# An S5 recurrence cut into chunks of four tokens, with powers of the transition in its matrices

## The chip, the cores and the metric

The kernel runs on one core of a Trainium2 chip. The metric is the device time of one execution in microseconds (us); the median of three runs of the kernel before is 2751.92 us (2749.49 to 2754.79).

## The reference

Two blocks of two layers each run over 256 tokens of width 1024. The first block has gated feed-forwards, an attention with an LRU, and a short-convolution mixer. The second block has, in each layer, a mixer of two groups (S5 and gated linear attention, GLA) and then a feed-forward (a dense one in its first layer, 8 experts with 2 chosen per token in its second). All weights are float32. The change touches the S5 group alone:

```python
# u: 256 tokens x 512 channels = 32 groups of 16 channels; 64 complex states per group
lam_bar = exp(lam * dt)                           # one complex factor per state
b_bar = ((lam_bar - 1) / lam)[..., None] * b_mat  # 64 x 16 per group
bu = einsum('gph,blgh->blgp', b_bar, u)
h[l] = lam_bar * h[l-1] + bu[l]                   # over all 256 tokens
y = einsum('ghp,blgp->blgh', c_mat, h).real + d_skip * u
y = gelu(y); y_s5 = y * sigmoid(y @ w_glu + b_glu)
```

A mixer is followed by a projection of both groups, a residual sum and a layer norm.

## The kernel before

The program is written out engine by engine with semaphores; nothing but the code's own order sets the order of the work. `SUBS` names ten stages: stages 6 and 8 (`mix2`) are the two S5 and GLA mixers, stages 5 and 7 are the feed-forwards ahead of them. Weights arrive by SP's queue in units (1 MB and 0.5 MB). ScalarE makes a rounded copy of each (`hi`, lines 395 and 402) and VectorE the rest of it (`lo_gu`, `lo_d`, lines 857 and 862), and TensorE does three products for one (`mm3`, lines 1721 to 1723). A feed-forward is a loop over such units.

A mixer goes so on TensorE (`mix2`, line 2009). First come the projections (`stream`, six units), with the eight levels of the GLA scores between them (`level`, line 2047, matrices of 64 rows that use one half of the array each, in turns). VectorE prepares each level (`differences`, `decayed`, lines 1242 to 1250) and takes it up (`masked`, lines 1258 to 1268), and does `lo` of the next units between. Then comes the recurrence, in eight rounds `r`, each of two state tiles (a tile is 128 states, that is two groups). `bu(r)` (line 2130) makes the input of the states, complex and 256 tokens long. VectorE turns it by a table `E` of powers of the transition's phase (`turn_in`, lines 1319 to 1322), joins the products (1339, 1340), scans four rows of 256 (1344) with the factor's size alone as decay, and turns back: two products on VectorE (`turn_back`, 1329 and 1330), two on GpSimd (1705, 1706). TensorE multiplies the four products with the C matrices (`CS`, line 2154, outputs of 32 rows). `skip` (1287) adds `d_skip * u`. In rounds 0 and 1 VectorE also does the GLA heads' norm (`gated_heads`, 1298; `mixed_heads`, through line 1091). TensorE puts the first row block of the projection (`r_[0]`) ahead of the last round.

GpSimd builds the tables `E` (16384 numbers a partition for 16 tiles, real and imaginary, `table`, lines 1617 to 1629) during stages 5 and 7, after the last `modulation` sums. In a mixer it fetches `s5_c`, waits for the GLA gate and multiplies it (1688), fetches the B matrices of each round (1691, 1696), and does its two products a round. `CS` is made by VectorE at the start of a mixer (1208 to 1214, seven instructions).

Of the kernel before, what the change touches and what calls it, by code (L numbers as in the profile page):

```python
# [22 lines left out]
F32 = mybir.dt.float32  # L23
# [22 lines left out]
LEVELS = (64, 32, 16, 8, 4, 2, 1)  # L46

# [52 lines left out]
def program(nc, A, out):  # L100
    with ExitStack() as ctx:
# [14 lines left out]
        XH, XL = sb("xT_hi", [P, KD, S], F32R), sb("xT_lo", [P, KD, S], F32R)  # L116
        MH, ML = sb("mixT_hi", [P, KD, S], F32R), sb("mixT_lo", [P, KD, S], F32R)
# [32 lines left out]
        def view(at, n):  # L150
# [12 lines left out]
        E = view(8192, 8192).rearrange("p (c t s) -> p c t s", c=2, t=16)  # L163
# [32 lines left out]
        SBM = [view(1024 + 512 * i, 512).rearrange("p (c t m) -> p c t m", c=2, t=2) for i in range(2)]  # L196
        CS = view(2048, 1536).rearrange("p (c t h) -> p c t h", c=3, t=16)
        CRAW = view(3584, 1024).rearrange("p (c t h) -> p c t h", c=2, t=16)
        CT = [view(4608 + 512 * i, 512).rearrange("p (t h) -> p t h", h=32) for i in range(2)]
        W = view(3584, 1024).rearrange("p (c t s) -> p c t s", c=2, t=2)  # L200
        PP = [view(4608 + 512 * i, 512) for i in range(4)]
        TURNED = [[ROW[:, 512 * i:512 * i + 512] for i in range(4)],
                  [ROW[:, 2048:2560], HG, first_net[:, 0:512], first_net[:, 512:1024]]]
# [25 lines left out]
        s5b_in, s5c_in = [sem(f"s5b_in{i}") for i in range(2)], sem("s5c_in")  # L229
# [26 lines left out]
            "table", "bu", "bu_used", "states", "prod", "prod2", "y", "ysum", "gelu", "yh", "yl", "sig", "gated")}  # L256
# [25 lines left out]
        def s5_input(r, c):  # L282

            return PA[:, 2 * ((r + 1) % 2) + c, :]
# [5 lines left out]
        def tile2(x):  # L290

            return x.rearrange("p a b -> p (a b)")

# [95 lines left out]
        def _(act):  # L389
# [127 lines left out]
            def ffn(n0, dyn, nf):  # L517
# [7 lines left out]

                if n0 == 0:
                    steps(0)
                with act.Fori(1 if n0 == 0 else 0, nf // 2) as j:
                    steps(dyn + j * 2)
# [114 lines left out]
            def mix2(b):  # L644
# [7 lines left out]
                def keep_u(t, used, count):  # L652
                    act.wait_ge(used, count)
                    act.activation(UT[:, t, :], PA[:, t % 2, 0:S], ACT.Copy).then_inc(g["u_sb"], 1)
# [20 lines left out]
                decay(1)  # L675
                act.wait_ge(d_used, U + 3)
# [7 lines left out]
                decay(6)  # L684
                keep_u(0, gu_used, U + 5)
# [15 lines left out]
                act.activation(grs, gss, ACT.Sqrt, bias=eps_rms, scale=1.0 / P).then_inc(g["root"], 1)  # L701
# [1823 lines left out]
```

## Time and profile before

| | us |
|---|---|
| median of three runs | 2751.92 |
| span of the profiled execution | 2747.2 |
| TensorE busy in it | 2600.3 (95%) |
| VectorE busy | 2165.5 (79%) |
| ScalarE busy | 1483.6 (54%) |
| GpSimd busy | 947.8 (34%) |

The span runs from the first to the last instruction of the profiled execution; the page gives no other time of that execution, and the runs' median is 4.7 us above it. The chain that ended last is to 38% of the span TensorE's; the rest of it lies on no other engine for more than 1%. The two recurrences lie at 1136 to 1208 us and at 1566 to 1638 us. In them TensorE is busy for 51.4 of 72 us and VectorE for 70.4.

### The profile page before, as it was taken

To read this page: it belongs to the slowest core of one execution; us is meant where nothing else is said; L and a number is where in the kernel's file an instruction comes from. 1 tells how busy PE (TensorE), PEld (TensorE's weight loads), DVE (VectorE), ACT (ScalarE), POOL (GpSimd) and SP (SyncE) were. 2 spreads that over 40 slices of the span, in tenths; PEclk is the share of its full clock that TensorE was granted. 3 is DMA by queue.
4 is the path that set the end of the run, shared out by engine and by line. 5 is a ranking of instruction groups with operands and counts; after the bars stand their busy time and mean duration, and the time that the engine had idled before them with its cause. 6 is when DMAs were issued, how large, how long until landed. Compare 5 with 4: busy or idle time off the path is not lost. (4 is left out here: it accounts for less than half of the span.)

```text
span 2747.2 us, 47482 instructions
## 1 busy us (share of the span) xinstructions
PE 2600.3 (95%) x17802; PEld 2379.0 (87%) x17802; DVE 2165.5 (79%) x2488; ACT 1483.6 (54%) x1930; POOL 947.8 (34%) x586
## 2 busy tenths in 40 slices
PE   8999899999998998888998978999999999999997
PEld 7999699999897998658998747999999999999986
DVE  5667666766787676987855997898989898989888
ACT  4337543443434334424334515777777777777765
POOL 6990089688789992126900130000000000000000
PEclk9999999999999998999999988999999999999999
DMA  8664267566566653324553415999999999999985
GB/s 309 252 237 148 103 241 256 202 250 254 191 241 229 220 183 134 115 105 164 183 184 138 164 63 192 343 350 333 352 335 349 338 347 343 347 345 346 340 320 216
DMA packets 129209, 670.58 MB, mean 244 GB/s; under 512 B 14672, under 2 KB 14992, under 8 KB 80064
## 3 DMA queue, kind: packets, MB, share of 16 engines
q1 hardware_dynamic: 111024, 604.72, 59.9%
q0 software_dynamic: 18064, 64.21, 6.9%
q8 instruction: 81, 1.33, 0.2%
q14 instruction: 40, 0.33, 0.0%
HBM read 667.82 MB, written 1.05 MB: 243 GB/s over the span
## 5 line engine op out<-in xcount | busy, mean ns | idle before, releaser
L1721 PE MATMUL work<-xT_hi,wh_gu 128*128 128x256 f32 x2088 | 593.9, 284 | 21.6 <-DVE xT_lo L985 12.0
L1722 PE MATMUL work<-xT_lo,wh_gu 128*128 128x256 f32 x2088 | 592.3, 284 | 0.0
L1723 PE MATMUL work<-xT_hi,wl_gu 128*128 128x256 f32 x2088 | 591.7, 283 | 0.0
L1721 PE MATMUL work<-wh_gu,mixT_hi 128*128 128x256 f32 x1792 | 507.5, 283 | 2.8 <-DVE wl_gu L1439 1.5
L1722 PE MATMUL work<-wl_gu,mixT_hi 128*128 128x256 f32 x1792 | 505.8, 282 | 0.0
L1723 PE MATMUL work<-wh_gu,mixT_lo 128*128 128x256 f32 x1792 | 505.5, 282 | 0.0
L857 DVE TENSOR_TENSOR wl_gu<-raw_gu,wh_gu 128x2048 fp32r<-128x2048 f32 x158 | 392.3, 2483 | 72.0 <-ACT wh_gu L395 71.5
L1721 PEld LDWEIGHTS work<-xT_hi,wh_gu 128*128 128x128 f32 x2088 | 401.3, 192 | 30.1 <-issue 21.3
L1722 PEld LDWEIGHTS work<-xT_lo,wh_gu 128*128 128x128 f32 x2088 | 401.7, 192 | 4.8
L1723 PEld LDWEIGHTS work<-xT_hi,wl_gu 128*128 128x128 f32 x2088 | 401.5, 192 | 0.0
L862 DVE TENSOR_TENSOR wl_d<-raw_d,wh_d 128x1024 fp32r<-128x1024 f32 x157 | 250.2, 1594 | 189.6 <-ACT wh_d L402 189.5
L1721 PE MATMUL acc<-wh_d,h_hi 128*128 128x512 f32 x912 | 380.4, 417 | 2.8 <-DVE wl_d L1444 2.7
L1723 PE MATMUL acc<-wh_d,h_lo 128*128 128x512 f32 x912 | 361.2, 396 | 0.0
L1722 PE MATMUL acc<-wl_d,h_hi 128*128 128x512 f32 x912 | 361.1, 396 | 0.0
L1721 PEld LDWEIGHTS work<-wh_gu,mixT_hi 128*128 128x128 f32 x1792 | 340.9, 190 | 12.5 <-DVE wl_gu L1439 1.7
L1722 PEld LDWEIGHTS work<-wl_gu,mixT_hi 128*128 128x128 f32 x1792 | 341.6, 191 | 8.8
L1723 PEld LDWEIGHTS work<-wh_gu,mixT_lo 128*128 128x128 f32 x1792 | 341.5, 191 | 0.0
L402 ACT ACTIVATE wh_d<-raw_d 128x1024 fp32r<-128x1024 f32 x157 | 166.2, 1059 | 276.1 <-PE acc L1723 276.1
L395 ACT ACTIVATE wh_gu<-raw_gu 128x2048 fp32r<-128x2048 f32 x158 | 300.7, 1903 | 25.4 <-PE acc L1723 25.0
L1652 POOL TENSOR_SCALAR scratch<-scratch,small 128x1024 f32<-128x1024 f32 x84 | 312.9, 3724 | 4.2
L1439 DVE TENSOR_TENSOR wl_gu<-raw_gu,wh_gu 128x2048 fp32r<-128x2048 f32 x113 | 259.1, 2293 | 38.0 <-ACT wh_gu L726 37.9
L1439 DVE TENSOR_TENSOR wl_gu<-scratch,wh_gu 128x2048 fp32r<-128x2048 f32 x112 | 256.6, 2291 | 25.5 <-ACT wh_gu L726 25.0
(436 smaller groups left out, 4785.6 us busy)
## 6 DMA issues: line engine op xcount, KB each, us to landing
raw_gu<-in_w_gu SPq DMA_DIRECT2D x271, 1024.0 KB, 5.2
raw_d<-in_w_d SPq DMA_DIRECT2D x269, 512.0 KB, 5.4
scratch<-in_w_gu SPq DMA_DIRECT2D x112, 1024.0 KB, 7.2
scratch<-in_w_d SPq DMA_DIRECT2D x112, 512.0 KB, 7.8
scratch<-in_w_mod POOLq DMA_DIRECT2D x96, 512.0 KB, 3.7
scratch<-in_s_b POOLq DMA_DIRECT2D x16, 256.0 KB, 2.9
rows<-in_norm_post POOLq DMA_DIRECT2D x6, 512.0 KB, 4.4
rows<-in_ln_g POOLq DMA_DIRECT2D x4, 512.0 KB, 5.5
```

The costliest lines, as they stand in the source:

```text
L395: act.activation(wh_gu[k][:, :, :, :].rearrange("p a k n -> p (a k n)"), raw_gu[k][:, :], ACT.Copy).then_inc(gu_hi, 1)
L402: act.activation(wh_d[k][:, :], raw_d[k][:, :], ACT.Copy).then_inc(d_hi, 1)
L857: TT(wl, raw_gu[k][:, :], wh.bitcast(F32), ALU.subtract).then_inc(gu_lo, 1)
L862: TT(wl_d[k][:, :], raw_d[k][:, :], wh_d[k][:, :].bitcast(F32), ALU.subtract).then_inc(d_lo, 1)
L1439: TT(wl, RAW_GU[k] if k > 1 else RAW_GU[k][:, :], wh.bitcast(F32), ALU.subtract).then_inc(gu_lo, 1)
L1652: link(pool.tensor_scalar(MW[n % 3], MW[n % 3], c, None, ALU.mult))
L1721: pe.matmul(out_, w[0], m[0], start=start, stop=False)
L1722: pe.matmul(out_, w[0], m[1], start=False, stop=False)
L1723: return pe.matmul(out_, w[1], m[0], start=False, stop=stop)
```

## The change

`PH` = 4 tokens form a chunk, so there are `NC` = 64 chunks. The 256 tokens are kept by phase: ScalarE writes `u` as 4 blocks (phase) of 64 (chunk) (`keep_u`), and the output is put back in order when the mixer's result is written.

- The input of a chunk's state is the sum over its four tokens of (power of the transition) times B times u. GpSimd makes the powers of B in the feed-forward ahead (`input_powers`, 18 operations of 128 x 512), from rows that TensorE has spread out there (`transition_rows`, 32 products) and ScalarE has copied. TensorE's `inputs(half)` has 64 products of 32 rows into 128, 64 columns each; the four state tiles of a set use the array's four row blocks. All of it is two halves, not eight rounds.
- The scans run over chunks with the decay's fourth power. VectorE has `states(half)` and `turn_back(half)`, operations of 1024 or 512 a partition, and one scan of 1024 (16 rows of 64, each begun afresh by a zero in the decay). ScalarE fills the decays (`decays`, 8 small operations a half).
- The output of a token is C times (power) times the state of the chunk before (`outputs(t)`, 32 products of 32 x 64 for each `t`) and a short convolution inside the chunk (`nearby(t)`, four products). Its kernel is TensorE's `kernels()` (128 products of 32 x 32), copied by ScalarE into a block form that GpSimd has zeroed (`kernel_blocks`).
- The C matrices' powers are made by GpSimd at the start of each mixer (`output_powers`, 30 operations of 128 x 512), in place of VectorE's seven, and ahead of the gate's product. GpSimd's two products a round and the B fetches in the mixer are gone; the B matrices are fetched whole, by eight DMAs, before. The table has 64 places in place of 256.

```diff
+PH = 4
+NC = S // PH
...
+                if n0 in (START[5], START[7]):
+                    ahead, l = 2, 1 + (n0 == START[7])
+                    steps(0)
+                    act.wait_ge(s["bt_ps"], l)
+                    act.activation(BST.rearrange("p c t h -> p (c t h)"), tile2(PB[:, 2:4, :]), ACT.Copy).then_inc(s["bt_sb"], 1)
+                    steps(2)
+                    act.wait_ge(s["lam_ps"], l)
+                    act.activation(LAM.rearrange("p c x -> p (c x)"), tile2(PB[:, 2:4, :]), ACT.Copy).then_inc(s["lam_sb"], 1)
...
+                    act.activation(UT[:, t, :].rearrange("p (f c) -> p f c", f=PH),
+                                   PA[:, t % 2, 0:S].rearrange("p (c f) -> p f c", f=PH),
+                                   ACT.Copy).then_inc(g["u_sb"], 1)
...
+                def decays(half):
+
+                    act.wait_ge(s["bpow"], n + 1)
+                    act.wait_ge(s["fresh"], n + 1)
+                    per = DEC[:, half].rearrange("p (j c t x) -> p j c t x", j=4, c=2, t=2)
+                    for j in range(4):
+                        for t in range(2):
+                            at = 16 * n + 8 * half + 4 * t + j
+                            last = act.activation(per[:, j, :, t, :], fresh_start.unsqueeze(1).broadcast_to([P, 2, NC]),
+                                                  ACT.Copy, scale=s5p[:, 1, at:at + 1])
+                    last.then_inc(s["dec"], 1)
...
+                def kernel_blocks():
+
+                    act.wait_ge(s["kern"], n + 1)
+                    act.wait_ge(s["kzero"], n + 1)
+                    for j in range(4):
+                        r = slice(32 * j, 32 * j + 32)
+                        act.activation(NEARBY[r, :, :, r], PB[r, 3, :].rearrange("p (t d h) -> p t d h", t=4, d=PH),
+                                       ACT.Copy).then_inc(s["kd"], 1)
...
-                TT(CT[0], CRAW[:, 0], cr, ALU.mult)
-                link(TT(CT[1], CRAW[:, 1], ci, ALU.mult))
-                TT(CS[:, 0], CT[0], CT[1], ALU.subtract)
-                link(TT(CS[:, 1], CT[1], CT[0], ALU.subtract))
-                TT(CT[0], CRAW[:, 0], ci, ALU.mult)
-                link(TT(CT[1], CRAW[:, 1], cr, ALU.mult))
-                link(STT(CS[:, 2], CT[0], -1.0, CT[1], ALU.mult, ALU.subtract))
...
+                def states(half):
+
+                    er, ei = turn(half)
+                    v, w, wa, wb = s5_input(half), pairs(W), pairs(WA), pairs(WB)
+                    dve.wait_ge(s["bu"], 2 * n + half + 1)
+                    if half == 0:
+                        dve.wait_ge(s["table"], n + 1)
+                    TT(wa, v, er, ALU.mult)
+                    link(TT(wb, v, ei, ALU.mult))
+                    TT(w[:, :, 0], wa[:, :, 0], wb[:, :, 1], ALU.add).then_inc(s["bu_used"], 1)
+                    link(TT(w[:, :, 1], wa[:, :, 1], wb[:, :, 0], ALU.subtract))
+                    dve.wait_ge(s["dec"], 2 * n + half + 1)
+                    dve.tensor_tensor_scan(W, DEC[:, half], W, 0.0, ALU.mult, ALU.add).then_inc(s["states"], 1)
...
+                def turn_back(half):
+
+                    er, ei = turn(half)
+                    w, wa, wb = pairs(W), pairs(WA), pairs(WB)
+                    dve.wait_ge(s["states"], 2 * n + half + 1)
+                    TT(wa, w, er, ALU.mult)
+                    link(TT(wb, w, ei, ALU.mult))
...
+                    TT(h[:, 0, :, :, 1:NC], cut[0][:, :, 0], cut[1][:, :, 1], ALU.subtract)
+                    link(TT(h[:, 1, :, :, 1:NC], cut[0][:, :, 1], cut[1][:, :, 0], ALU.add))
+                    dve.memset(small[:, 4:5], 0.0).then_inc(s["prod"], 1)
+
+                states(0)
+                gated_heads()
+                turn_back(0)
+                states(1)
+                mixed_heads()
+                turn_back(1)
+                skip(0)
+                skip(1)
                 lo_gu(U + 7)
+                skip(2)
                 skip(3)
                 lo_d(U + 7)
...
+            def input_powers(n):
+
+                pool.wait_ge(s["lam_sb"], n + 1)
+                pool.wait_ge(s5b_in, 128 * (n + 1))
+                lr, li = LAM[:, 0], LAM[:, 1]
+                t = ET[:, 0:512]
+                for k in range(1, PH):
+                    (r0, i0), (r1, i1) = ((BP[:, x, 0], BP[:, x, 1]) for x in (k - 1, k))
+                    TT(r1, r0, lr, ALU.mult)
+                    link(TT(t, i0, li, ALU.mult))
+                    link(TT(r1, r1, t, ALU.subtract))
+                    TT(i1, r0, li, ALU.mult)
+                    link(TT(t, i0, lr, ALU.mult))
+                    link(TT(i1, i1, t, ALU.add))
...
+            def output_powers(n):
+
+                def of(i):
+                    return s5p[:, i, 16 * n:16 * n + 16].unsqueeze(2).broadcast_to([P, 16, 32])
+                cr, ci, t = CRAW[:, 0], CRAW[:, 1], CTMP
+                pool.wait_ge(s5c_in, 16 * (n + 1))
+                for d in range(PH + 1):
...
+                    b0, b1 = CP[d - 1][:, 0], CP[d - 1][:, 1]
+                    TT(c0, b0, of(0), ALU.mult)
+                    link(TT(t, b1, of(18), ALU.mult))
+                    link(TT(c0, c0, t, ALU.add))
+                    TT(c1, b1, of(0), ALU.mult)
+                    link(TT(t, b0, of(18), ALU.mult))
+                    link(TT(c1, c1, t, ALU.subtract))
+                    if d >= PH - 1:
+                        pool.memset(small[:, 6:7], 0.0).then_inc(s["cpow"], 1)
...
+                    output_powers(n)
...
+            def input_columns(n):
+
+                pe.wait_ge(s5b_in, 128 * (n + 1))
+                for c in range(2):
+                    for t in range(4):
+                        last = pe.transpose(PB[:, 2 + c, t * P:(t + 1) * P], BP[:, 0, c, t * P:(t + 1) * P], ident)
+                last.then_inc(s["bt_ps"], 1)
+
+            def transition_rows(n):
+
+                pe.wait_ge(par_ready, 1)
+                for c, i in enumerate((0, 18)):
+                    for t in range(4):
+                        for j in range(4):
+                            at = 16 * n + 4 * t + j
+                            last = pe.matmul(PB[32 * j:32 * j + 32, 2 + c, t * P:(t + 1) * P],
+                                             s5p[:, i, at:at + 1].broadcast_to([P, 32]), ident, start=True, stop=True)
...
+                ahead = 0
+                if n0 in (START[5], START[7]):
+                    ahead, l = 1, int(n0 == START[7])
+                    input_columns(l)
+                    for r in (2, 3):
+                        gate_up(n0 + r)
+                        down(n0 + r - 1, 0, f0 + r - 1, 0, False, False)
+                    pe.wait_ge(s["bt_sb"], l + 1)
+                    transition_rows(l)
...
+                def inputs(half):
+
+                    if half == 0:
+                        pe.wait_ge(s["bpow"], n + 1)
...
+                    for t in (2 * half, 2 * half + 1):
+                        for c in range(2):
+                            for f in range(PH):
+                                for j in range(4):
+                                    r, at = slice(32 * j, 32 * j + 32), (4 * c + t) * NC
+                                    last = pe.matmul(PA[:, j, at:at + NC], BP[r, PH - 1 - f, c, t * P:(t + 1) * P],
+                                                     UT[r, t, f * NC:(f + 1) * NC], start=f == 0, stop=f == PH - 1)
                     last.then_inc(s["bu"], 1)
 
-                bu(0)
+                def kernels():
+
+                    pe.wait_ge(s["bt_sb"], n + 1)
+                    pe.wait_ge(s["cpow"], 2 * n + 1)
+                    for t in range(4):
+                        for d in range(PH):
+                            for c in range(2):
+                                for j in range(4):
+                                    at = (PH * t + d) * 32
+                                    last = pe.matmul(PB[32 * j:32 * j + 32, 3, at:at + 32], BST[:, c, 4 * t + j, :],
+                                                     CP[d][:, c, 4 * t + j, :], start=c == 0, stop=c == 1)
+                    last.then_inc(s["kern"], 1)
+
+                def nearby(t):
+
+                    for d in range(PH):
+                        pe.matmul(s5_output(t)[:, d * NC:S], NEARBY[:, t, d, :], UT[:, t, 0:S - d * NC], start=d == 0, stop=False)
+
+                def outputs(t):
+
+                    half = t // 2
+                    pe.wait_ge(s["prod"], 2 * n + half + 1)
+                    for f in range(PH):
+                        for c in range(2):
+                            for j in range(4):
+                                last = pe.matmul(s5_output(t)[32 * j:32 * j + 32, f * NC:(f + 1) * NC],
+                                                 CP[f + 1][:, c, 4 * t + j, :], HS[half][:, c, 2 * j + t % 2, :],
+                                                 start=False, stop=(f, c) == (PH - 1, 1))
+                    last.then_inc(s["y"], 1)
+
+                r_ = [row_of(k) for k in (6, 7, 4, 5, 3, 0, 1, 2)]
+                inputs(0)
                 heads()
-                bu(1)
+                kernels()
+                inputs(1)
...
+                nearby(0)
+                nearby(1)
+                outputs(0)
+                outputs(1)
+                pe.wait_ge(mix_l, MSTART[b] + 2)
+                nearby(2)
+                nearby(3)
+                pe.wait_ge(gu_lo, U + 7)
+                pe.wait_ge(s["bu_used"], 2 * (n + 1))
+                r_[0](U + 6, 0).then_inc(gu_used, 1)
+                outputs(2)
+                outputs(3)
```

TensorE in the first mixer, from the last GLA level (line 2047) on; before, word for word (`rows` are the scores or the turned products, `acc` and `work` the two halves of PSUM):

```order
L2047 MATMUL work<-scratch 128x128 x8
L2130 MATMUL acc<-scratch 128x256 x4
L2105 MATMUL work<-rows 128x128
L2106 MATMUL work<-rows 128x128
L2107 MATMUL work<-rows 128x128
...
L2130 MATMUL acc<-scratch 128x256 x4
L2114 MATMUL work<-const,scratch 128x128 x8
L2130 MATMUL acc<-scratch 128x256 x4
L2154 MATMUL work<-rows,scratch 32x256 x8
L2130 MATMUL acc<-scratch 128x256 x4
L2154 MATMUL work<-rows,scratch 32x256 x2
L2154 MATMUL work<-const,scratch 32x256 x2
```

Three rounds' inputs went ahead of the first outputs. Now, at the same place (line 2179 is the last GLA level, 2262 `inputs`, 2237 to 2239 the heads, 2275 `kernels`, 2246 the heads' transposes, 2282 `nearby`, 2291 `outputs`):

```order
L2179 MATMUL work<-scratch 128x128 x8
L2262 MATMUL acc<-scratch 128x64 x64
L2237 MATMUL work<-rows 128x128
...
L2275 MATMUL work<-scratch,mixT_hi_plain 32x32 x24
L2275 MATMUL work<-mixT_lo_plain,mixT_hi_plain 32x32 x8
...
L2262 MATMUL acc<-scratch 128x64 x64
L2246 MATMUL work<-const,scratch 128x128 x8
L2282 MATMUL work<-scratch 128x256
L2282 MATMUL work<-scratch 128x192
...
L2291 MATMUL work<-rows,scratch 32x64 x16
L2291 MATMUL work<-rows,mixT_lo_plain 32x64 x8
L2291 MATMUL work<-rows,mixT_hi_plain 32x64 x8
```

What were 4 products of 256 columns a round are now 64 of 64 columns a half, and the 128 small products of the kernels stand between the two halves' inputs.

GpSimd at the start of the first mixer, before:

```order
L1630 MEMSET small 128x1
L1682 DMA rows<-in_head_gain 128x512
L1683 DMA w_alpha<-in_w_alpha 16x256
L1685 DMA scratch<-in_s_c 128x1024
L1688 TENSOR_TENSOR const<-const,rows 128x1024
L1691 DMA scratch<-in_s_b 128x512 x2
L1696 DMA scratch<-in_s_b 128x512
```

And now (1795 to 1798 are the same three fetches; 1724 to 1737 are `output_powers`, of which the first seven operations stand here):

```order
L1795 DMA rows<-in_head_gain 128x512
L1796 DMA w_alpha<-in_w_alpha 16x256
L1798 DMA scratch<-in_s_c 128x1024
L1799 MEMSET scratch 128x64
L1800 MEMSET scratch 128x1
L1724 TENSOR_TENSOR scratch<-scratch,s5p 128x512
L1725 TENSOR_TENSOR mixT_lo_plain<-scratch,s5p 128x512
L1726 TENSOR_TENSOR scratch<-scratch,mixT_lo_plain 128x512
L1727 TENSOR_TENSOR scratch<-scratch,s5p 128x512
L1728 TENSOR_TENSOR mixT_lo_plain<-scratch,s5p 128x512
L1729 TENSOR_TENSOR scratch<-scratch,mixT_lo_plain 128x512
L1732 TENSOR_TENSOR scratch<-scratch,s5p 128x512
```

Nothing stood between the fetch of C and the gate's product (line 1688 before); now 30 operations of 128 x 512 do.

## Rows read from the trace of the kernel before

**Rows 1.** Stretches: length, busy us (count) of PE, PEld, DVE, ACT, POOL; clock, DMA:

```profile
937.00:1048.00 111.00, 111.00 (x783) 104.01 (x783) 83.55 (x67) 42.26 (x39) 105.38 (x114) 1.00 0.54 189
1074.00:1136.00 62.00, 61.78 (x452) 54.33 (x452) 49.59 (x78) 34.47 (x42) 4.01 (x4) 0.97 0.39 145
1136.00:1208.00 72.00, 51.41 (x241) 30.90 (x238) 70.38 (x114) 9.26 (x23) 24.09 (x22) 0.88 0.13 45
1504.00:1566.00 62.00, 61.63 (x450) 54.20 (x452) 54.17 (x82) 34.26 (x42) 5.10 (x6) 0.97 0.41 149
1566.00:1638.00 72.00, 51.37 (x242) 30.87 (x238) 70.51 (x114) 9.39 (x23) 24.07 (x22) 0.88 0.14 45
```

**Rows 2.** Waits, 1136 to 1208 us: who waited for whom, us, times, longest:

```profile
PE work L2154 <- DVE rows L1330: 13.9, 5, 3.4
```

**Rows 3.** Timeline of TensorE: start, us, operation [idle before]:

```profile
1135.02 1.16 PE L2047 MATMUL work<-scratch 64*128 64x128 f32 x16
1136.11 1.99 PE L2130 MATMUL acc<-scratch 128*128 128x256 f32 x8
1138.07 0.49 PE L2105 MATMUL work<-rows 128*128 128x128 f32 x2
...
1140.85 1.89 PE L2130 MATMUL acc<-scratch 128*128 128x256 f32 x8
1149.15 1.97 PE L2114 MATMUL work<-const,scratch 128*128 128x128 f32 x8 [6.41 <-DVE scratch L1298]
...
1201.84 0.50 PE L1721 MATMUL acc<-wh_gu,mixT_hi 128*128 128x512 f32 x1
...
1205.18 1.02 PE L2154 MATMUL work<-rows,scratch 128*32 128x256 f32 x4 [0.31 <-POOL const L1706]
```

**Rows 4.** Line 2047 alone: durations in ns, min/median/max, first and last start:

```profile
L2047 PE MATMUL work<-scratch x256: 272/272/373, 1097.2 to 1566.0; 64*128 64x128 f32 x128
```

**Rows 5.** Timeline of VectorE in the recurrence and behind it:

```profile
1140.66 0.69 DVE L1339 TENSOR_TENSOR scratch<-scratch 128x512 f32<-128x512 f32 x1
...
1141.98 2.44 DVE L1344 TENSOR_TENSOR_SCAN scratch<-s5p,scratch 128x256 f32<-128x256 f32 x4
...
1146.94 2.16 DVE L1298 SCALAR_TENSOR_TENSOR scratch<-work,small,const 128x128 f32<-128x128 f32 x8
...
1157.95 1.28 DVE L1091 TENSOR_TENSOR mixT_lo<-work,mixT_hi 128x512 fp32r<-128x512 f32 x2
...
1208.00 0.48 DVE L1287 SCALAR_TENSOR_TENSOR scratch<-scratch,cols,work 128x256 f32<-128x256 f32 x1 [0.81 <-PE work L2154]
...
1210.70 1.23 DVE L1361 TENSOR_TENSOR xT_lo<-scratch,xT_hi 128x1024 fp32r<-128x1024 f32 x1 [1.09 <-ACT xT_hi L710]
```

**Rows 6.** Timeline of GpSimd while the table is built:

```profile
984.46 1.04 POOL L1618 TENSOR_TENSOR scratch<-scratch,s5p 128x512 f32<-128x512 f32 x1
...
988.82 3.09 POOL L1621 TENSOR_TENSOR scratch<-scratch,s5p 128x512 f32<-128x512 f32 x1
991.99 1.29 POOL L1622 TENSOR_TENSOR scratch<-scratch 128x512 f32<-128x512 f32 x1
```

**Rows 7.** Timeline of VectorE in the same stretch:

```profile
987.88 3.13 DVE L857 TENSOR_TENSOR wl_gu<-raw_gu,wh_gu 128x2048 fp32r<-128x2048 f32 x1
...
992.10 1.47 DVE L1072 TENSOR_TENSOR h_lo<-scratch,h_hi 128x256 fp32r<-128x256 f32 x1
```

**Rows 8.** Timeline of VectorE in the projections of the stage:

```profile
1087.05 2.29 DVE L857 TENSOR_TENSOR wl_gu<-raw_gu,wh_gu 128x2048 fp32r<-128x2048 f32 x1 [6.63 <-ACT wh_gu L395]
...
1090.39 0.69 DVE L1208 TENSOR_TENSOR scratch<-scratch,s5p 128x512 f32<-128x512 f32 x1
...
1104.54 0.42 DVE L1249 TENSOR_TENSOR scratch<-scratch 128x256 f32<-128x256 f32 x1
```

**Rows 9.** Timeline of GpSimd, the DMA of the C matrices:

```profile
1076.01 0.55 POOL L1685 DMA_DIRECT2D scratch<-in_s_c  x1 [6.35 <-DVE xT_lo L985]
```

**Rows 10.** DMA issues: KB each, median us to landing:

```profile
scratch<-in_s_c POOLq DMA_DIRECT2D x2, 512.0 KB, 3.9
```

More of the change, by code:

```diff
@@ L684, in mix2 @@
                 decay(6)
+                decays(1)
                 keep_u(0, gu_used, U + 5)
@@ new lines, in pairs, with turn @@
+                def pairs(x):
+                    return x.rearrange("p (j c y) -> p j c y", j=4, c=2)
+                def turn(half):
+                    return (E[:, c, half].rearrange("p (j y) -> p j y", j=4).unsqueeze(2).broadcast_to([P, 4, 2, 2 * NC])
+                            for c in range(2))
+                def states(half):
[10 more added lines that the diff above has]
+                    dve.tensor_tensor_scan(W, DEC[:, half], W, 0.0, ALU.mult, ALU.add).then_inc(s["states"], 1)
@@ L1630, in table @@
-                pool.memset(small[:, 6:7], 0.0).then_inc(s["table"], 1)
+                turns = E.rearrange("p c h (o x) -> p c (h o) x", o=8)
+                pool.memset(turns[:, 0, :, 0:1], 1.0)
+                pool.memset(turns[:, 1, :, 0:1], 0.0)
+                for c, i in enumerate((11, 10)):
+                    last = pool.tensor_copy(pw[:, c].rearrange("p (h j t) -> p h j t", h=2, j=4),
+                                            s5p[:, i, 16 * n:16 * n + 16].rearrange("p (h t j) -> p h j t", h=2, t=2))
@@ new lines, in table, with squared @@
+                link(last)
+                def squared():
+                    TT(t0, pw[:, 0], pw[:, 0], ALU.mult)
+                    link(TT(t1, pw[:, 1], pw[:, 1], ALU.mult))
+                    link(TT(pw[:, 1], pw[:, 0], pw[:, 1], ALU.mult))
+                    TT(pw[:, 0], t0, t1, ALU.subtract)
+                    link(TT(pw[:, 1], pw[:, 1], pw[:, 1], ALU.add))
+                squared()
+                squared()
+                w = 1
+                while w < NC:
+                    pr, pi = (pw[:, c].unsqueeze(2).broadcast_to([P, 16, w]) for c in range(2))
+                    et = ET[:, 0:16 * w].rearrange("p (t s) -> p t s", t=16)
+                    re0, im0 = turns[:, 0, :, 0:w], turns[:, 1, :, 0:w]
+                    re1, im1 = turns[:, 0, :, w:2 * w], turns[:, 1, :, w:2 * w]
+                    TT(re1, re0, pr, ALU.mult)
+                    link(TT(et, im0, pi, ALU.mult))
+                    link(TT(re1, re1, et, ALU.subtract))
+                    TT(im1, re0, pi, ALU.mult)
+                    link(TT(et, im0, pr, ALU.mult))
+                    link(TT(im1, im1, et, ALU.add))
+                    w *= 2
+                    if w < NC:
+                        squared()
```

221 lines of the change are left out of this document (82 added, 139 removed).

## The prediction

> **What bounds the kernel now.** I read the busy time by stretch first. In the feed-forward ahead of the first mixer TensorE is busy for 111.0 of 111 us, in the projections of both mixers for 61.8 and 61.6 of 62, in the two recurrences for 51.4 of 72 only; there VectorE is busy for 70.4 and 70.5 of 72 [rows 1]. So outside the recurrences a microsecond more on TensorE is a microsecond of the kernel, and in them VectorE sets the pace. The waits say the same: in the first recurrence TensorE waits 13.9 us for VectorE's second turned product [rows 2] and 6.4 us for its gated heads [rows 3]. A recurrence lasts from 1136.11 us, the first `bu`, to 1208.48, the end of the last `skip` [rows 3, 5]: 72.4 us, and what stands behind it waits for it.
>
> **The recurrence, new: TensorE.** Let p be the time between two matmul records when small products follow each other in different parts of the array. A float32 product is two records (8 products are x16 [rows 3]). A recurrence then has 2 x 128 records of `inputs`, 256 of `kernels` and 4 x 64 of `outputs`: 768p. Beside them stand the heads, 1138.07 to 1140.85, 2.8 us; their transposes, 2.0; four `nearby`, each 640 columns, where 1024 columns took 1136.11 to 1138.07, so 1.2 each and 4.9 together; one row block, 1201.84 to 1204.87, 3.0; one `skip` at the end, 0.5 [rows 3, 5]. Sum 13.2 + 768p, against 72.4: a recurrence gets shorter by 59.2 - 768p, if TensorE is then its bound.
>
> Is it? VectorE: an operation of 512 is 0.69 us, one of 1024 is 1.23, a scan of 1024 as four of 256, 2.44 [rows 5]. `states` is 2 x 1.23 + 2 x 0.69 + 2.44 = 6.3, `turn_back` 2 x 1.23 + 2 x 0.69 and small memsets, 3.9. Behind the second `inputs` it owes 6.3 + 1.3 (`mixed_heads`) + 3.9 = 11.5 us until `outputs(2)`; TensorE has 2.0 + 4.9 + 3.0 + 128p = 9.9 + 128p to do in that time, more than 11.5 from p = 0.013 on. So VectorE falls from bound to second. ScalarE's kernel blocks and GpSimd's memset lie beside `inputs(1)`; `decays` on ScalarE, 16 small operations, lie in the projections, where it is busy for 34.5 of 62 us [rows 1]. I cost these at nothing; without that cover a few us each.
>
> What is p? No row shows four parts in turns with so few columns. The nearest is line 2047: two halves of the array in turns, 16 records from 1135.02 to 1136.11, 0.068 each with the change-over, (1.16 - 0.27) / 15 = 0.059 without [rows 3, 4]. The heads, in one part, take 2.78 / 24 = 0.116 a record. So two parts run side by side at 0.116 / 2. If four do too, p = 0.029; if the sequence of instructions is what limits, p stays at 0.059, and with change-overs 0.068. Fewer columns (32 or 64, not 128) argue for the lower end, four times as many instructions in a row as any row has for the upper. I take the middle of 0.029 and 0.059, p = 0.044: 33.8 + 13.2 = 47.0 us, so 25.4 us less for each recurrence; the ends give 36.9, 13.9 and 7.0 (at 0.068) less.
>
> A rule of the Trainium skill speaks to this. "TensorE: Matmul & The Clock Gate", section "Wait — 56ns, not 53.3ns?", has two floors for small matmuls: about 25 ns between starts, and about 62 ns for each where the engine's sequencer decodes in its software. The rows' 0.059 is between them and decides neither. By the first the sum below would come to about -43 us, by the second to +19.
>
> **New on TensorE in the feed-forwards.** Eight transposes (as the heads', 2.0 us [rows 3]) and 32 products, 64p = 2.8: 4.8 us a layer. TensorE has no idle time there [rows 1], so they count in full. Bounds 3.9 and 6.4.
>
> **New on GpSimd, and what it does to VectorE.** In the feed-forwards it loses the table's long steps and gets 18 operations; VectorE has pauses there (83.6 of 111 us busy with GpSimd busy for 105.4) and TensorE does not wait for it [rows 1]: nothing. In the mixers it is another matter. `output_powers` starts when C has landed, 1076.0 + 3.9 = 1080 [rows 9, 10], and is 20 products of 1.04 us and 10 sums of 1.29 [rows 6], 34 us if nothing is in the way. These lie on the projections, where GpSimd now works for 4 us [rows 1] and VectorE has a chain that TensorE follows closely. While the table was built the two engines held each other up: a product of GpSimd took 3.09 us in place of 1.04, while VectorE's `wl_gu` ran, itself 3.13 in place of 2.29; `h_lo`, of 256 places, took 1.47, where such an operation takes 0.42 [rows 6 to 8]. So an operation of VectorE that reads two tiles of SBUF and meets one of GpSimd waits for about 0.84 to 1.05 us. In the projections nearly all of them read two. 30 meetings of 1.0 are 30 us a layer. Against that stands VectorE's slack: 62 - 49.6 = 12.4 in the first mixer, 62 - 54.2 = 7.8 in the second, and the seven operations for `CS` that go, 7 x 0.69 = 4.8 [rows 1, 8]. Late by 30 - 17.2 = 12.8 and 30 - 12.6 = 17.4, together 30 us, and late here is late for TensorE: each level waits for `decayed`, and behind the level in its queue stand the next unit's products. Bounds: 0 if GpSimd always yields; 39 if every meeting costs the whole operation (68 - 29.8, rounded up). I take 30.
>
> **The sum**, on the profiled execution's 2747.2 us: 2 x (13.2 + 768p - 72.4) + 2 x (2.0 + 64p) + 30 = 1664p - 84.4. At p = 0.044 that is -11. The median of the runs is 4.7 us over the span; I leave that as it is: 2752 - 11 = 2741. It is nothing at p = 0.051.
>
> **Rivals.**
> - *The sequence of small instructions is the bound* (p 0.059 to 0.068, from 0.051 it decides). Place: `inputs`, `kernels` and `outputs`, 1536 records in both layers. For it: nothing in the trace goes faster for long than 0.059; against it: there two parts reach exactly twice one part's pace, so the array, not the sequence, seems to limit. The sum: +14 to +29, 2766 to 2781.
> - *Four parts run side by side* (p = 0.029): -36, 2716. For it the same exact halving.
> - *GpSimd yields* and costs VectorE some 8 us and not 30, at p = 0.044: -33, 2719. Against it 3.13 and 1.47 in the rows.
> - *The change moves the bound and gains nothing*: TensorE is by then in the recurrence for what VectorE was, within 5.5 us in all, p near 0.051.
> - TensorE's clock is granted at 0.88 in the recurrence [rows 1], so some of it at 1.2 and not 2.4 GHz. If the thin products get it for all of it, the 13.2 us of wide work in each grow by up to 13.2, less what they have now; I keep that for the upper end.
>
> **How the numbers follow.** Forecast, some -25 to -6 us: 0.34. Four parts side by side or a yielding GpSimd: 0.22. No change: 0.08. Slow sequence, with or without a slow clock: 0.36. What a measurement of this kernel tells from no change is 0.2%, 5.5 us. So faster 0.56, same 0.08, slower 0.36. The range for 8 in 10 takes in p = 0.029 with half the loss on GpSimd (-51) and p = 0.059 to 0.068 (+14 to +29): 2702 to 2778. The likeliest case has 2727 to 2747 for itself.
>
> **What would show it.** In the profile after: records of `inputs`, `kernels` and `outputs` 0.03 to 0.06 us apart; the recurrence 40 to 55 us long with TensorE nearly always at work; VectorE's short operations in the projections at 1.2 to 1.5 us, and 10 us and more of TensorE's idle time before the levels, more in the second mixer; 4 to 6 us more in each feed-forward. I am wrong if the records stand 0.06 or more apart, if VectorE's 0.42 us stay 0.42 beside GpSimd, or if VectorE's halves, not TensorE, end the recurrence.

## The result, and the profile after

The kernel before takes 2752.4 us (median of 4 runs), the changed one 2726.3 (4 runs, 2723.6 to 2730.9): a ratio of 0.9898, 95% interval 0.9883 to 0.9913, 26 us less. The forecast was 11 less. The profiled executions are 2747.2 and 2728.8 us long, 18.4 apart; these two stand at the fast end of one group of runs and at the slow end of the other.

I cut both traces at the same events: `xT_lo` of a mixer (VectorE), its first `inputs` or `bu` (TensorE), and the `xT_lo` behind its last `skip`. Lengths in us:

| stretch | before | after | difference | forecast |
|---|---|---|---|---|
| start to first mixer's `xT_lo` | 1071.81 | 1077.64 | +5.8 | +4.8 |
| projections 1 | 64.30 | 79.44 | +15.1 | +12.8 |
| recurrence 1 | 74.60 | 38.02 | -36.6 | -25.4 |
| rest of mixer 1, norm | 36.01 | 36.02 | 0.0 | 0 |
| feed-forward between | 255.24 | 267.06 | +11.8 | +4.8 |
| projections 2 | 64.28 | 83.21 | +18.9 | +17.4 |
| recurrence 2 | 74.60 | 37.86 | -36.7 | -25.4 |
| rest | 1106.41 | 1109.57 | +3.2 | 0 |

How far one profile may be trusted: until the first cut the changed kernel and six of the kernels below run the same instructions, and that stretch was 1071.3 to 1078.6 us long in their seven profiles. A few microseconds there or in the rest are no finding, the +5.8 of the first row included. Where the code is the same, the projections repeat within about 2 us, the first recurrence within 1 (37.0 to 38.0) and the second within 3 (35.1 to 37.9). The busy times by stretch, of the changed kernel (columns as in [rows 1]):

```profile
1077.64:1157.08 79.44, 65.34 (x452) 56.72 (x452) 64.93 (x75) 41.18 (x63) 48.58 (x36) 0.91 0.30 106
1157.08:1195.10 38.02, 33.97 (x858) 31.21 (x856) 29.75 (x42) 13.66 (x30) 2.92 (x3) 0.82 0.19 67
1498.17:1581.38 83.21, 67.78 (x453) 58.90 (x453) 72.57 (x79) 41.19 (x63) 47.46 (x38) 0.86 0.29 105
1581.38:1619.24 37.86, 31.22 (x858) 28.49 (x856) 29.65 (x42) 13.54 (x30) 2.92 (x3) 0.91 0.23 82
```

and the same two stretches of projections of the kernel before:

```profile
1071.81:1136.11 64.30, 61.89 (x453) 54.34 (x453) 51.89 (x82) 36.74 (x47) 4.01 (x4) 0.95 0.38 140
1501.95:1566.23 64.28, 61.87 (x452) 54.31 (x452) 56.45 (x86) 36.51 (x47) 5.10 (x6) 0.95 0.39 144
```

VectorE (third busy time) works 13 and 16 us longer in the projections, with seven operations fewer. TensorE's waits, in the projections of the first and of the second mixer (who waited for whom, us, times, longest):

```profile
PE work L2198 <- DVE scratch L1306: 7.4, 1, 7.4
PE work L2179 <- DVE scratch L1306: 3.8, 1, 3.8
...
PE work L2198 <- DVE scratch L1306: 7.2, 1, 7.2
PE work L2179 <- DVE scratch L1306: 4.7, 1, 4.7
```

Line 1306 is `decayed`, lines 2179 and 2198 the levels that follow it: 11 to 12 us of waiting a layer, none before. On VectorE a `decayed` beside a power on GpSimd, and a `differences` of the same shape after the last power (what was 0.42 us in [rows 8] is 0.42 only where GpSimd rests); then one of GpSimd's operations beside `wl_gu` (1.04 us alone, [rows 6]):

```profile
1118.34 1.26 DVE L1306 TENSOR_TENSOR scratch<-scratch 128x256 f32<-128x256 f32 x1
...
1144.62 0.42 DVE L1298 TENSOR_TENSOR scratch<-scratch 128x256 f32<-128x256 f32 x1
```

```profile
1093.14 2.98 POOL L1732 TENSOR_TENSOR scratch<-scratch,s5p 128x512 f32<-128x512 f32 x1
```

TensorE in the first recurrence (start, length, records; in brackets the idle time ahead, where "issue" means that nothing in the profile released it). This is the stretch that answers to [rows 3]:

```profile
1157.08 3.80 PE L2262 MATMUL acc<-scratch 32*128 32x64 f32 x128
...
1163.69 0.60 PE L2275 MATMUL work<-scratch,mixT_hi_plain 128*32 128x32 f32 x46
...
1167.04 0.53 PE L2275 MATMUL work<-scratch,mixT_hi_plain 128*32 128x32 f32 x38 [1.99 <-issue]
...
1170.77 6.67 PE L2262 MATMUL acc<-scratch 32*128 32x64 f32 x120 [2.06 <-issue]
1177.38 1.97 PE L2246 MATMUL work<-const,scratch 128*128 128x128 f32 x8
1179.14 3.97 PE L2282 MATMUL work<-scratch 128*128 128x256 f32 x16
1183.04 0.65 PE L2291 MATMUL work<-rows,scratch 128*32 128x64 f32 x32
```

The distance between two records is here 0.028 us in `inputs(0)` ((3.80 - 0.27) / 127, the length of the last taken off), (0.60 - 0.20) / 45 = 0.009 in `kernels`, (0.65 - 0.22) / 31 = 0.014 in `outputs`. Twice TensorE stands still for 2 us with nothing to wait for. From 1168.5 us, shortly after the first gap, to 1182.1 the granted clock is 0.50, its lower level (1.2 GHz), and behind the second gap 120 records of `inputs(1)` take 6.67 us, where at the full clock it would be 3.6:

```profile
1170.00:1177.00 7.00, 6.23 (x116) 6.23 (x120) 4.69 (x10) 2.35 (x4) 0.14 (x1) 0.50 0.02 5
```

VectorE in the same stretch ([rows 5] before):

```profile
1160.95 1.23 DVE L1378 TENSOR_TENSOR xT_hi_plain<-acc,scratch 128x1024 f32<-128x1024 f32 x1 [1.92 <-PE acc L2262]
...
1168.61 0.20 DVE L1349 RECIPROCAL small<-small 128x8 f32<-128x8 f32 x1 [1.65 <-ACT small L762]
...
1177.51 1.22 DVE L1378 TENSOR_TENSOR xT_hi_plain<-acc,scratch 128x1024 f32<-128x1024 f32 x1 [2.67 <-PE acc L2262]
...
1192.40 0.48 DVE L1343 SCALAR_TENSOR_TENSOR scratch<-scratch,cols,work 128x256 f32<-128x256 f32 x1 [0.41 <-PE work L2291]
```

From 1160.95 to the second half's turn-back at 1188.4 it has two short pauses: `inputs(1)` came 2.67 us late because of TensorE's gaps and its clock, ScalarE's root for the heads 1.65 late. TensorE waits for no other engine in this recurrence; its busy 33.97 us and the two gaps (1.99 and 2.06) are the whole 38.02. In the second recurrence it is otherwise. There TensorE has one gap, `inputs(1)` goes at the full clock in 3.87 us, and TensorE then waits for VectorE's `mixed_heads`:

```profile
1606.30 4.96 PE L2282 MATMUL work<-scratch 128*128 128x256 f32 x16 [4.63 <-DVE mixT_lo L1158]
```

So the first is as long as TensorE alone makes it, and in the second the chain goes through VectorE, at almost the same 38 us. In the feed-forward between the mixers TensorE waits for the DMAs of the second layer's B, which are issued only at 1244.68, behind `x_done` and the norm's rows:

```profile
1255.94 1.97 PE L1918 MATMUL work<-const,scratch 128*128 128x128 f32 x8 [6.46 <-DMA scratch<-in_s_b]
```

### The profile page after: what moved, and what is told of

It is laid out like the page before. It is cut to its first block, busy times and chain, and to the rows that moved or that the text cites. A ratio compares the mean times of both kernels' runs of the same rounds, so it can differ in the third digit from the quotient of the medians.

```text
span 2728.8 us, 50009 instructions
## 1 busy us (share of the span) xinstructions
PE 2581.1 (95%) x19162; PEld 2392.5 (88%) x19162; DVE 2100.9 (77%) x2330; ACT 1502.7 (55%) x1974; POOL 937.1 (34%) x590
## 4 chain that ended last, share of the span: by engine, by line
PE 77%; DVE 10%; POOL 6%; ACT 3%; issue 2%; DMA 1%; DVEq 0%; POOLq 0%; ACTq 0%
PE work L1823 15%; PE work L1824 15%; PE work L1825 15%; PE acc L1823 8%; PE acc L1825 8%; PE acc L1824 8%; POOL scratch L1761 3%; POOL scratch L1762 2%; DVE wl_gu L919 1%; PE work L2368 1%; DVE wl_d L924 1%; PE acc L2428 1%; PE work L1881 1%; DVE mixT_lo L1158 1%; PE work L1910 1%
## 5 line engine op out<-in xcount | busy, mean ns | idle before, releaser
L1823 PE MATMUL work<-xT_hi,wh_gu 128*128 128x256 f32 x2088 | 596.0, 285 | 22.5 <-DVE xT_lo L1052 12.1
L1823 PEld LDWEIGHTS work<-wh_gu,mixT_hi 128*128 128x128 f32 x1792 | 341.2, 190 | 12.8 <-DVE wl_gu L1492 1.7
L1492 DVE TENSOR_TENSOR wl_gu<-raw_gu,wh_gu 128x2048 fp32r<-128x2048 f32 x113 | 259.1, 2293 | 37.9 <-ACT wh_gu L788 37.8
```

What stands on the lines that cost most here:

```text
L1492: TT(wl, RAW_GU[k] if k > 1 else RAW_GU[k][:, :], wh.bitcast(F32), ALU.subtract).then_inc(gu_lo, 1)
L1823: pe.matmul(out_, w[0], m[0], start=start, stop=False)
```

## The experiments

**Parts in a row.** Do the parts of the array really work side by side? The same products, one part after the other:

```diff
-                            for f in range(PH):
-                                for j in range(4):
+                            for j in range(4):
+                                for f in range(PH):
```

and likewise in `kernels` and `outputs`.

> The changed kernel with the loops of inputs, kernels and outputs turned so that all products of one part of the array come one after the other, then those of the next part; the same products in the same number. Theory: the short records (0.030 us in inputs, 0.009 in kernels, 0.014 in outputs) come from four parts working side by side. In a row they are then 0.12, 0.036 and 0.056 apart; inputs(0), 3.7 us from first to last record, takes 15; the recurrence, 38 us, takes 60 to 75; the kernel about 45 to 75 us more, some 2775 to 2800. Rival: the records are short because the products are thin, and the parts have nothing to do with it: nothing changes, 2726.

Measured: 2774 us (2 runs, ratio to before 1.008), the recurrences 59.6 and 62.6 us, 22 and 25 longer than in the changed kernel. `inputs(0)` is

```profile
1158.18 11.90 PE L2262 MATMUL acc<-scratch 32*128 32x64 f32 x128
```

in place of 3.80. The mean of 0.09 a record mixes two clocks: 0.065 until 1162.8 us, at the full clock, and 0.12 behind it, where the granted clock is 0.50. At the full clock a record in a row is thus 2.3 times as far from the next as in turns in `inputs` (0.065 for 0.028), 2.9 times in `kernels` (0.026 for 0.009) and 3 times in `outputs` (0.044 for 0.014), less than the four that I expected (0.12, 0.036 and 0.056). The parts do run side by side, if not four times as fast as in a row, and the interleaved order is worth some 46 us to the change (21.6 + 24.7, the lower clock included): written this way it would have lost.

**Thin inputs.** What sets the pace of one part? Of B's 128 columns only 32 are used (the rest of the result stays as it was):

```diff
-  pe.matmul(PA[:, j, at:at + NC], BP[r, PH - 1 - f, c, t * P:(t + 1) * P],
+  pe.matmul(PA[r, j, at:at + NC], BP[r, PH - 1 - f, c, t * P:t * P + 32],
```

> The changed kernel with inputs' weights cut from 128 columns to 32 (a quarter of B's rows is used, the rest of the result is left as it was, so the output is wrong); same number of products, same 64 moving columns, still four parts in turns. Theory: a record's distance in one part follows from the columns of the weights plus the moving ones (0.12 for 128 + 64, 0.056 for 32 + 64, 0.036 for 32 + 32), and four parts share it: inputs goes from 0.030 to 0.014 us a record, 128 records from 3.7 to 1.8 us. Rival: the distance is set by how few rows of the array (32 of 128) work in each product, since outputs and kernels use all 128: it stays at 0.030. The kernel's time: 1 to 4 us less by the first, since VectorE waits for inputs(0) and (1).

```profile
1153.06 1.99 PE L2262 MATMUL acc<-scratch 32*32 32x64 f32 x128
```

(1.99 - 0.21) / 127 = 0.014, to the digit that of `outputs`, which has the same columns and four times the rows. Rows don't matter, columns do. How the columns of the weights and the moving ones go together this run can't say: the sum of both, as I expected, and the wider of the two both give 0.014. The recurrences are 34.3 and 35.3 us, the kernel 2725 (2 runs), not told apart from 2726.

**Kernels twice.** What are the idle gaps?

```diff
-                    for t in range(4):
+                    for t in (0, 1, 2, 3, 0, 1, 2, 3):
```

> The changed kernel with the 256 records of kernels issued twice, the second time over the same result. Theory: TensorE's idle gaps of 2.0 us without a releaser come when its instructions are used faster than they are fetched; 256 of its instructions are 16 KB, the size of one packet of the instruction queue, and the gaps stood 128 records (256 instructions) apart. 512 instructions more then cost 2.4 us of records and two more gaps of 2 us, 6 to 7 us between heads and inputs(1) in each layer. Rival: the gaps belong to a place in the program, not to the pace: their number stays, and it costs 2.4 us a layer.

The rows that have a gap ahead of them, first recurrence:

```profile
1159.17 0.53 PE L2275 MATMUL work<-scratch,mixT_hi_plain 128*32 128x32 f32 x38 [1.73 <-issue]
...
1162.90 0.76 PE L2275 MATMUL work<-scratch,mixT_hi_plain 128*32 128x32 f32 x40 [2.43 <-issue]
...
1166.90 0.76 PE L2275 MATMUL work<-scratch,mixT_hi_plain 128*32 128x32 f32 x40 [2.06 <-issue]
...
1170.36 6.68 PE L2262 MATMUL acc<-scratch 32*128 32x64 f32 x120 [0.99 <-issue]
```

Four gaps in place of two, 3.7 us, 4.0 and 3.5 from one to the next; the second recurrence has three in place of one. The recurrences are 7.1 and 5.7 us longer, as the theory had it, and not 2.4. The kernel's median is 2744.6 (8 runs), 18.3 us over the changed one. Six of the eight runs took 2742 to 2747 us, two 2733, and the profile (span 2730.9) is of one of these two; what the other six have more stays open, and I read the stretches. The DMA traffic of this burst, 1156 to 1172 us in slices of 0.4 us, is packets of the instruction queue and nothing else, five of 16 KB:

```profile
GB/s 0 41 0 0 0 0 0 0 0 0 0 41 0 0 0 0 0 0 0 0 0 41 0 0 0 0 0 0 0 0 41 0 0 0 0 0 0 0 41 0
...
q8 instruction: 5, 0.08, 2.0%
```

They stand as far apart as the gaps, one for each 128 records, and each of the first four starts 2.3 to 2.7 us ahead of the record that ends a gap (1156.47 and 1159.17, 1160.53 and 1162.90, 1164.54 and 1166.90, 1168.03 and 1170.36). So a short burst goes at 0.009 us a record, but a long one at 3.7 / 128 = 0.029 on average: TensorE's instructions are used up faster than they come. What paces the packets themselves no run shows.

**Powers left out, powers early, powers on VectorE.** Three ways to take `output_powers` off GpSimd in the projections: 24 of its 30 operations left out; all 30 done in the feed-forward ahead; all 30 on VectorE.

```diff
 # powers_left_out
-                for d in range(PH + 1):
+                for d in range(1):
 # powers_early, for both layers
                         table(0)
+                        output_powers(0)
...
-                    output_powers(n)
+                    pool.dma_start(view(2048, 2048), view(5120, 2048)).then_inc(s5c_in, 16)
+                    pool.dma_start(view(4096, 1024), view(15360, 1024)).then_inc(s5c_in, 16)
 # powers_on_vector, in mix2 of VectorE
                 lo(U + 2)
+                power(0)
+                power(1)
...
                 lo(U + 3)
+                power(2)
...
                     masked(j)
+                    if j in (1, 4):
+                        power({1: 3, 4: 4}[j])
```

> The changed kernel with 6 of the 30 GpSimd operations of output_powers; the four further powers are not computed (the first one stands in for them, so the state's part of the output is wrong). Theory: VectorE and GpSimd hold each other up in the projections, 15.1 us late in the first mixer and 18.9 in the second. Without 24 of 30 operations VectorE's short operations are 0.42 us again behind about 1094 us, TensorE's waits of 12 us a layer before the levels go, and with the seven VectorE operations for CS gone too the projections are as long as before the change: some 30 to 34 us less, 2693 to 2697. Rival: the lateness comes from ScalarE's 16 decays in the same stretch, or from C landing late: it stays, 2726. Halfway (a lateness in proportion to the operations without a slack) would be 27 us, 2699; the slack says most of it goes.

> The changed kernel, complete, with the 30 operations of output_powers moved to the feed-forward ahead, behind the table on GpSimd, into places that are free there; two DMAs bring three of the five products into their places when the mixer starts. Theory: in the feed-forward VectorE has pauses (busy 84 of 111 us) that take the contention, and the projections are as before the change: 34 us less in all, 2692, at most 5 us given back in the feed-forwards. Rival: contention only moves: TensorE waits for h_lo and wl in the feed-forward instead, and the gain is under 10 us.

> The changed kernel, complete, with the 30 operations of output_powers on VectorE itself (12 ahead of the alpha, 6 behind the third unit, 6 each behind the second and the fifth level's mask), none on GpSimd. Theory: 30 operations of 0.69 us are 20.7 us on VectorE, less than what contention costs it; over its slack (12.4 + 4.8 and 7.8 + 4.8) 3.5 and 8.1 us late, so some 22 us less than the changed kernel, 2704. Rival: the operations stand in the chain that TensorE follows and the slack lies elsewhere, so that most of the 20.7 us shows: 2726 or more.

Left out: 2695.0 us (4 runs, ratio 0.9791, interval 0.9770 to 0.9813). Early: 2694.3 (0.9795, 0.9776 to 0.9814). On VectorE: 2727.5 (0.9915, 0.9894 to 0.9936), no gain at all over the changed kernel. The first mixer's projections with the powers early, and with them on VectorE:

```profile
1074.87:1140.11 65.24, 62.31 (x453) 54.72 (x453) 47.40 (x75) 41.18 (x63) 3.73 (x5) 0.94 0.40 147
```

```profile
1078.24:1157.81 79.57, 65.90 (x452) 57.32 (x452) 67.87 (x107) 41.28 (x63) 3.20 (x4) 0.91 0.30 107
```

The first two confirm the theory and its rivals fall: contention it was (ScalarE's decays are still there, busy 41.18), and in the feed-forward it costs nothing, which is as long as it was (266.95 against 267.06). The third refutes my slack: 3.5 and 8.1 us late by it, measured 15.3 in either mixer (79.57 and 79.55 for 64.30 and 64.28). VectorE is busy for 47.4 us without the powers, 67.9 with them as its own work, 64.9 with them on GpSimd. So 30 operations on the other engine cost VectorE 17.5 us (20.5 in the second mixer, 72.57 - 52.06), as good as doing them itself (20.5), and of the 17.5 only 3.3 are absorbed: the stretch grows by 14.2 (of the 20.5 in the second mixer 2.9, it grows by 17.6).

**B's DMAs early.**

```diff
                     pool.wait_ge(s["y"], 4 * (n + 1))
+                    if n == 0:
+                        input_matrix(1)
```

> The changed kernel with the eight DMAs of the second layer's input matrix issued at the end of the first mixer, when its second inputs have been read, not in the feed-forward behind x_done and the DMAs of the norm's rows. Theory: TensorE's wait of 6.5 us before input_columns in the second feed-forward goes, and nothing comes in its place: the feed-forward is 5 us longer than before the change and not 11.8; 6 to 7 us less, 2720. [...]

Measured 2723.6 us (4 runs, ratio 0.9895, interval 0.9875 to 0.9915): in the medians not told apart from 2726.3, in the stretch it is: 258.31 us for 267.06, 8.7 less. Of these 6.5 are the wait; I put the rest down to the clock behind it, granted at 0.50 from 1253.8 to 1260.6 us in the changed kernel and in full here. The transposes and the transition's products stand there at the full clock:

```profile
1251.32 1.03 PE L1919 MATMUL work<-const,scratch 128*128 128x128 f32 x8
```

```profile
1269.36 1.95 PE L1929 MATMUL work<-const,s5p 128*32 128x128 f32 x64
```

and the feed-forward is 3.1 us longer than before the change.

**Reordered.** Both of these, and the recurrence in another order:

```diff
                 states(0)
-                gated_heads()
                 turn_back(0)
+                gated_heads()
 ...
                 heads()
-                kernels()
                 inputs(1)
+                kernels()
 ...
+                outputs(2)
+                outputs(3)
                 pe.wait_ge(gu_lo, U + 7)
                 pe.wait_ge(s["bu_used"], 2 * (n + 1))
                 r_[0](U + 6, 0).then_inc(gu_used, 1)
-                outputs(2)
-                outputs(3)
```

> A version meant to be the best, complete: output_powers early, as in the run before, the second input matrix's DMAs at the end of the first mixer, and the recurrence in another order: VectorE turns back the first half before it gates the heads (it waited 1.65 us for ScalarE's root there), TensorE does inputs(1) before kernels (so that the gaps of its instruction stream fall behind it) and outputs(2) and (3) before the row block. Theory: from 2694, 8 us less for the DMAs' wait, and each recurrence 5 us shorter (37.2 and 35.1 to about 31): 2676 to 2680. Rival: the kernel blocks now come later (their gap, GpSimd's memset and ScalarE's copies stand behind kernels), TensorE waits for them with nearby(0), and the recurrences stay at 35 to 37: 2686.

2683.4 us (5 runs, ratio 0.9761, interval 0.9744 to 0.9777), between the two forecasts. The recurrences went from 37.2 and 35.1 to 32.9 and 34.4: the first by 4.3, the second by 0.7 only, which is within its spread. The end of the first mixer, where B's DMAs are now issued, is 1.3 us longer (37.34 for 36.01). The gap still stands, now behind `inputs(1)`, and `nearby(0)` waits for the blocks made from `kernels`, as the rival said:

```profile
1151.45 0.53 PE L2286 MATMUL work<-scratch,mixT_hi_plain 128*32 128x32 f32 x38 [1.69 <-issue]
...
1157.12 4.29 PE L2293 MATMUL work<-scratch 128*128 128x256 f32 x16 [1.41 <-ACT scratch L715]
```

**Fewer kernels.** That version, with `kernels` as 64 products for 128 and B's DMAs behind the norm's rows:

```diff
-  pe.matmul(PB[32*j:32*j+32, 3, at:at + 32], BST[:, c, 4*t+j, :], CP[d][:, c, 4*t+j, :], ...)   # d = 0..3
+  pe.matmul(PB[32*j:32*j+32, 3, at:at + 96], BST[:, c, 4*t+j, :], three[:, :, c, 4*t+j, :], ...)
+  pe.matmul(PB[32*j:32*j+32, 3, at:at + 32], BST[:, c, 4*t+j, :], CP[3][:, c, 4*t+j, :], ...)
```

> The reordered version, complete, with two more changes: kernels as 64 products in place of 128 (three of the four powers lie side by side and are the 96 moving columns of one product, the fourth keeps its own of 32), and the second input matrix's DMAs behind those of the norm's rows. Theory: with 256 instructions fewer between inputs(1) and the heads' transposes TensorE's instruction stream is not used up; the idle gap of 1.7 to 2.0 us without a releaser goes, kernels take 2 us and not 4.2, nearby(0) starts 2 us earlier, and each recurrence is 1 to 1.5 us shorter (then VectorE ends it); the first mixer's end is back at 36.0 us. 3 to 4 us less than the reordered version's 2683: 2680. Rival: the gap has nothing to do with the number of instructions: it stays at its place, and only the records are fewer: kernels 3.5 us, the kernel 2682 to 2683.

```profile
1150.51 0.54 PE L2286 MATMUL work<-scratch,mixT_hi_plain 128*32 128x96 f32 x16
...
1152.23 0.31 PE L2291 MATMUL work<-mixT_lo_plain,mixT_hi_plain 128*32 128x32 f32 x16
1155.85 1.17 PE L2256 MATMUL work<-const,scratch 128*128 128x128 f32 x8 [3.31 <-DVE scratch L1358]
...
1166.78 0.65 PE L2307 MATMUL work<-rows,scratch 128*32 128x64 f32 x32 [1.09 <-DVE small L1403]
```

`kernels` takes 2.0 us and the gap is gone (in the second mixer 0.4 us of it is left). What TensorE gains there it waits for VectorE, ahead of the transposes and of `outputs(2)`: both recurrences are 32.9 us, so the first gains nothing and the second 1.4. VectorE is the bound again. The first mixer's end is back at 36.20 us. 2678.9 us (5 runs, ratio 0.9741, interval 0.9728 to 0.9755), the fastest of all: 72 us less than the kernel before, 47 less than the changed one. Of the 4.2 us between the profiles of this version and the reordered one, 2.8 lie in the rest, where the code is the same.

## Why the prediction was off by fifteen microseconds

- **The step that failed is the term 2 x 768p of the recurrence.** I chose p = 0.044 from two ends, for all three kinds of product alike. Measured: 0.028 in `inputs`, 0.009 in `kernels`, 0.014 in `outputs`; that is 7.1 + 2.3 + 3.6 = 13.0 us of records for 33.8, a mean of 0.017, below even my lower end. The mechanism was right in kind (the parts work side by side; parts in a row shows it, with a factor of 2.3 to 3), and so was the lower end, 0.029, for products with weights as wide as those of the rows. What I missed is that the weights of the other two are 32 columns wide, not 128, and that a record is then shorter: 0.014 for 0.028 with weights of 32 columns for 128 (thin inputs). I had written that fewer columns argue for the lower end and then took the middle.
- The recurrence did not fall to 13.2 + 13.0 = 26.2 us, but to 35.8 as I counted it (1157.08 to 1192.88). Almost all of the 9.6 us more is TensorE's own: its two gaps are 4.1, `inputs(1)` at the lower clock is 3.6 more, the four `nearby` are 1.4 more (6.3 for 4.9), partly at that clock too. No row of the kernel before shows such gaps; the lower clock was there before ([rows 1] has 0.88), and I had kept it for the upper end. In the second recurrence one gap is gone, and TensorE waits 4.63 us for VectorE instead: with 0.014 in `outputs` TensorE's 9.9 + 1.8 = 11.7 us stand against VectorE's 11.5, so which of the two sets the end was nearly a toss. This error hid half of the first one. Net -36.6 and -36.7 for -25.4 each: 22.5 us of the difference.
- **B's DMAs.** I counted each queue's operations but not when the second layer's eight are issued. TensorE's wait, with its clock, is 8.7 us. The products in the feed-forward I had at 4.8, they are 3.0 (1.03 + 1.95): p is 0.027 there, and the 2.0 for eight transposes came from a row that stands at a granted clock of 0.50 (1149.15 us, [rows 3]); at the full clock they take 1.03.
- **GpSimd beside VectorE:** 30 forecast, 34.1 measured, and still the working was wrong twice. 30 meetings cost 17.5 and 20.5 us, not 30; the slack is 3 us, not 17.2 and 12.6. The errors cancel, and that this sum came out was luck. The mean of a stretch (62 us less the busy time) is no slack where another engine follows every step of the chain.
- Nothing for the table, the decays, the blocks and the memset on ScalarE and GpSimd: held. The last mix, now written in another order, takes 2.14 us on VectorE for 1.23, and TensorE doesn't wait for it (36.01 and 36.02 us).
- The rule that I weighed, "TensorE: Matmul & The Clock Gate", section "Wait — 56ns, not 53.3ns?" of the Trainium skill, gave -43 with its lower floor and +19 with its upper one. The recurrences' rows are nearer the lower one on average over a long burst (0.029) and far below it in a short one (0.009), and the upper floor was not seen here. So neither bounds products in different parts of the array in this kernel.

Summed by stretches: +5.8 +15.1 -36.6 +11.8 +18.9 -36.7 +3.2 = -18.5 in the two profiles, -26 in the medians. Against the forecast of -11 the recurrences are 22.5 less, and the rest 15 more (7.0 in the feed-forward between, 3.9 in the projections, 1.0 and 3.2 at both ends). The 8 us between the profiles and the medians lie in the spread of single executions; I did not find out what the 3 us in the rest are, and kernels twice, with the same code there, has 0.1.

## What to carry to other kernels

Price a small product by the wider of its own weights and its own moving operand, for each kind apart, and from a row at a known clock. Look at how many instructions in a row it takes: here bursts at 0.009 us a record ended after 136 and 244 records (68 and 122 float32 products) in a wait for instructions. An idle engine is not free if its operations and those of the one that sets the pace hold each other up: here 30 operations on GpSimd cost VectorE as much as doing them itself, and they belong into a stage where VectorE has pauses. Slack is what a chain of waits shows, not a stretch less its busy time.

## What the runs showed of the hardware that I had not expected

- Four parts in turns at the full clock, distance of two records times four, by columns of weights and moving: 32 and 32: 0.036 us; 32 and 64: 0.056; 32 and 96: 0.085; 32 and 128: 0.107; 128 and 64: 0.111. It goes by the wider of the two, 0.84 to 0.89 ns a column (1.1 at 32 and 32), and so do the heads, one part of 128 and 128, with 0.112 a record. The sum of both columns, as I took it in thin inputs, fits the first five with 0.56 to 0.67 ns a column, but not the heads (0.44). For 32 and 64 it is the same with 32 rows as with 128.
- TensorE's instructions arrive at about 128 records (a weight load and a product each) per 3.5 to 4.0 us, a packet of 16 KB. A burst that is faster stands still for 0.9 to 2.5 us, with nothing named that it waits for (in fewer kernels 0.4). Behind a first such gap the granted clock may fall to its lower level: 1.9 times as long for the next 120 records of `inputs`.
